# Modulation, x and the first products of a two-block transformer kernel, pair by pair instead of all at once

## The reference

```python
c_act = jax.nn.silu(c)                                     # (1, 1024)
mod = jnp.einsum('bd,de->be', c_act, w_ada[l]) + b_ada[l]   # (1, 6 * 1024)
sh1, sc1, g1, sh2, sc2, g2 = [m[:, None, :] for m in jnp.split(mod, 6, axis=-1)]
h = x * (1.0 + sc1) + sh1
proj = jnp.einsum('bsd,dk->bsk', h, w_in)
z, xbc, dt_raw, q, k, v, f_raw = jnp.split(proj, SPLITS, axis=-1)
```

## Time and profile before

| | |
|---|---|
| median of 3 runs | 1414.13 us (1413.6 to 1414.81) |
| the profiled execution, its own time | 1416.64 us |
| its span (first to last instruction) | 1414.9 us |
| instructions | 17285 |
| DMA | 158.58 MB, mean 112 GB/s |

### The profile page before, as it was taken

The page is one execution under the profiler, slowest core; times in us unless marked ns, Lnnn a source line. Parts: engine busy times, 40 slices in busy tenths (PEclk is TensorE's granted clock), DMA queues, the critical chain, the costliest instruction groups (busy, mean ns, idle before and its releaser), DMA issues.

```text
span 1414.9 us, 17285 instructions
## 1 busy us (share of the span) xinstructions
PE 1368.2 (97%) x6567; PEld 1123.8 (79%) x6567; DVE 692.2 (49%) x1005; ACT 547.8 (39%) x793; POOL 690.8 (49%) x544
## 2 busy tenths in 40 slices
PE   2999999999999999999999997999999999999999
PEld 2888788888878778888888886887788888888887
DVE  6676978789753672131325456348623213132231
ACT  0636445566663252231332316325525323142230
POOL 0453855432346664455445544754644445445442
PEclk9999999999999999999999999999999999999999
DMA  9353435655323433322232232343132322322231
GB/s 334 119 131 101 98 119 179 194 152 167 105 72 132 139 90 111 97 89 90 93 114 89 89 110 72 100 122 89 46 119 67 112 89 89 115 93 89 89 104 74
DMA packets 132248, 158.58 MB, mean 112 GB/s; under 512 B 9468, under 2 KB 93712, under 8 KB 131936
## 3 DMA queue, kind: packets, MB, share of 16 engines
q1 hardware_dynamic: 123760, 146.95, 33.2%
q10 hardware_dynamic: 6240, 5.40, 1.6%
q0 software_dynamic: 2192, 5.49, 1.2%
HBM read 153.47 MB, written 2.26 MB: 110 GB/s over the span
## 4 chain that ended last, share of the span: by engine, by line
PE 88%; DVE 5%; POOL 3%; ACT 1%; issue 1%; DMA 1%; SPq 0%; DVEq 0%; POOLq 0%; ACTq 0%
PE bank L1706 26%; PE bank L1707 26%; PE bank L1708 26%; POOL w_lo L551 3%; DVE tmp L1271 2%; PE bank L1845 2%; PE bank L1855 1%; DMA arena<-in_w_ada_dram 1%; PE bank L2223 1%; PE bank L2038 1%; PE bank L1830 1%; PE bank L1858 1%; PE bank L1820 1%; PE bank L2039 1%; PE bank L1982 1%
## 5 line engine op out<-in xcount | busy, mean ns | idle before, releaser
L551 POOL TENSOR_TENSOR w_lo<-raw,w_hi 128x512 fp32r<-128x512 f32 x428 | 588.5, 1407 | 601.1 <-ACT w_hi L745 599.9
L1706 PE MATMUL bank<-w_hi,a_hi 128*128 128x512 f32 x928 | 364.6, 393 | 8.3 <-DVE a_lo L1164 6.0
L1708 PE MATMUL bank<-w_hi,a_lo 128*128 128x512 f32 x928 | 361.9, 390 | 0.0
L1707 PE MATMUL bank<-w_lo,a_hi 128*128 128x512 f32 x928 | 361.9, 390 | 0.0
L745 ACT ACTIVATE w_hi<-raw 128x2048 fp32r<-128x2048 f32 x107 | 204.5, 1911 | 365.3 <-PE bank L1708 361.7
L1706 PE MATMUL bank<-a_hi,w_hi 128*128 128x512 f32 x800 | 316.4, 395 | 3.4 <-DVE a_lo L1164 2.5
L1707 PE MATMUL bank<-a_lo,w_hi 128*128 128x512 f32 x800 | 312.9, 391 | 0.0
L1708 PE MATMUL bank<-a_hi,w_lo 128*128 128x512 f32 x800 | 312.8, 391 | 0.0
L1706 PEld LDWEIGHTS bank<-w_hi,a_hi 128*128 128x128 f32 x928 | 174.7, 188 | 46.2 <-DVE a_lo L1164 6.2
L1708 PEld LDWEIGHTS bank<-w_hi,a_lo 128*128 128x128 f32 x928 | 174.6, 188 | 36.8
L1707 PEld LDWEIGHTS bank<-w_lo,a_hi 128*128 128x128 f32 x928 | 174.7, 188 | 35.5
(11 more groups left out here) (248 smaller groups left out, 1246.7 us busy)
## 6 DMA issues: line engine op xcount, KB each, us to landing
raw<-in_w_mlp_dram SPq DMA_DIRECT2D x32, 1024.0 KB, 5.2
raw<-in_w_in_dram SPq DMA_DIRECT2D x24, 1024.0 KB, 5.2
arena<-in_w_ada_dram SPq DMA_DIRECT2D x18, 1024.0 KB, 6.7
raw<-in_w_ff_in_dram SPq DMA_DIRECT2D x16, 1024.0 KB, 5.4
raw<-in_w_ff_out_dram SPq DMA_DIRECT2D x16, 1024.0 KB, 5.0
raw<-in_w_out_dram SPq DMA_DIRECT2D x12, 1024.0 KB, 5.3
raw<-in_w_in_dram SPq DMA_DIRECT2D x16, 512.0 KB, 5.6
arena<-in_w_ada_dram SPq DMA_DIRECT2D x3, 2048.0 KB, 17.9
```

The costliest lines, as they stand in the source:

```text
L551: last = pool.tensor_tensor(w_lo[:, u0 % 2, cols], raw[:, u0 % 2, cols], w_hi[:, u0 % 2, cols].bitcast(F32), ALU.subtract)
L1706: pe.matmul(out_, hi_a, hi_b, start=start, stop=False)
L1707: pe.matmul(out_, hi_a, lo_b, start=False, stop=False)
L1708: return pe.matmul(out_, lo_a, hi_b, start=False, stop=stop)
```

## The change

The early columns of w_ada are loaded and used in four pieces g = 0 to 3. Piece g holds 256 columns of shift and the 256 columns of scale for the same features, that is for feature tiles 2g and 2g + 1. It comes in four DMAs (upper and lower four row blocks, shift and scale), and the quarter of x with the same features comes ahead of it. Unit U_XBC and the time step's columns come between pieces 0 and 1.

On each engine the work goes pair by pair. DVE weighs piece g, waits for PE's column sums, makes four columns of `mod`, and makes `a_lo` of the two tiles; the casts of unit U_XBC stand behind the first weighing. ACT waits for its part of `mod` and makes `a_hi` and the rests of the two tiles. PE sums the columns of piece g, transposes the next quarter of x (into banks 3 to 6, used twice), and multiplies the two tiles: time step, n = 0 and n = 1. Bank 7 holds the sums. The result of a weighing lies in a buffer of its own (`weighed`) instead of `tmp`.

```diff
+X_BANKS = (3, 4, 5, 6, 3, 4, 5, 6)
+        weighed = view(17280, 2, 512)
 (SP, prelude)
-                for half in range(2):
-                    sp.dma_start(ada[:, 0, 4 * half:4 * half + 4], w_ada_v[:, 4 * half:4 * half + 4, 0:512]).then_inc(ada_half[half], 16)
-                for n in range(1, 4):
-                    sp.dma_start(ada[:, n], w_ada_v[:, :, n * 512:n * 512 + 512]).then_inc(ada_in[n], 16)
-                sp.dma_start(xtok, x_v).then_inc(x_in, 16)
-                columns(0, 0, U_XBC, w_in_v, C_XBC + P * XBC_ORDER[0])
-                sp.wait_ge(cleared, 3)
-                sp.dma_start(dt_raw[:, :, 0:16], w_in_v[:, :, C_DT:C_DT + 16]).then_inc(dt_in, 16)
-                sp.dma_start(dt_raw[:, :, 32:48], w_in_v[:, :, C_F:C_F + 16]).then_inc(dt_in, 16)
+                for g in range(4):
+                    sp.dma_start(xtok[:, :, 256 * g:256 * g + 256], x_v[:, :, 256 * g:256 * g + 256]).then_inc(x_in[g], 16)
+                    for half, signal in enumerate((ada_upper[g], ada_lower[g])):
+                        rows_ = slice(4 * half, 4 * half + 4)
+                        for m in range(2):
+                            col = 1024 * m + 256 * g
+                            sp.dma_start(ada[:, g, rows_, 256 * m:256 * m + 256], w_ada_v[:, rows_, col:col + 256]).then_inc(signal, 16)
+                    if g == 0:
+                        columns(0, 0, U_XBC, w_in_v, C_XBC + P * XBC_ORDER[0])
+                        sp.wait_ge(cleared, 3)
+                        sp.dma_start(dt_raw[:, :, 0:16], w_in_v[:, :, C_DT:C_DT + 16]).then_inc(dt_in, 16)
+                        sp.dma_start(dt_raw[:, :, 32:48], w_in_v[:, :, C_F:C_F + 16]).then_inc(dt_in, 16)
 (ACT)
-            act.wait_ge(mod_made, 1)
-            turned_affine(R_H, T_H, 0, lambda k: mod[:, 8 + k:9 + k], lambda k: mod[:, k:k + 1])
+            def first_rest(k):
+                act.wait_ge(a_hi_made, T_H + k + 1)
+                if k >= 2:
+                    act.wait_ge(a_lo_made, T_H + k - 1)
+                act.activation(tmp[:, k % 2], a_hi[0][:, k].bitcast(F32), ACT.Identity, scale=-1.0, bias=mod[:, k:k + 1]).then_inc(tile_made, 1)
+            for g in range(4):
+                act.wait_ge(mod_made, g + 1)
+                for k in (2 * g, 2 * g + 1):
+                    turned_hi(R_H, 0, k, X_BANKS[k], mod[:, 8 + k:9 + k], mod[:, k:k + 1])
+                    if k % 2:
+                        first_rest(k - 1)
+                first_rest(2 * g + 1)
             hi(U_XBC + 1)
 (DVE, start)
-                (one weigh per piece n, sums of all four, then mod, the casts of U_XBC, split_affine)
+                for g in range(4):
+                    before = [(ada_upper[g], 32)] + ([(col_mm, g - 1)] if g >= 2 else [])
+                    weigh(weighed[:, g % 2], lambda k: ada[:, g, k], before, ada_sum, (ada_lower[g], 32))
+                    if g == 0:
+                        dve.wait_ge(vecs_t, 1)
+                        dve.tensor_copy(vec[:].rearrange("p a b -> p (a b)"), bank[7][:, 0:256]).then_inc(vecs_made, 1)
+                        dve.wait_ge(vecs_made, 1)
+                        dve.wait_ge(landed[U_XBC % 2], 16)
+                        for half in range(2):
+                            cols = slice(1024 * half, 1024 * half + 1024)
+                            dve.tensor_copy(w_hi[:, U_XBC % 2, cols], raw[:, U_XBC % 2, cols]).then_inc(w_hi_made, 1)
+                    dve.wait_ge(col_mm, g + 1)
+                    sums, v = bank[7][:, 256 + 4 * g:260 + 4 * g], V_BADA + 2 * g
+                    dve.tensor_tensor(mod[:, 2 * g:2 * g + 2], sums[:, 0:2], v0[:, v:v + 2], ALU.add)
+                    dve.scalar_tensor_tensor(mod[:, 8 + 2 * g:10 + 2 * g], sums[:, 2:4], 1.0, v0[:, v + 8:v + 10], ALU.add, ALU.add)\
+                        .then_inc(mod_made, 1)
+                    for k in (2 * g, 2 * g + 1):
+                        dve.wait_ge(tile_made, M_H + k + 1)
+                        dve.scalar_tensor_tensor(a_lo[0][:, k], bank[X_BANKS[k]][:], mod[:, 8 + k:9 + k], tmp[:, k % 2], ALU.mult, ALU.add)\
+                            .then_inc(a_lo_made, 1)
 (PE; the loop over m and the 32 transposes in one go are gone)
+            def turn_x(g):
+                pe.wait_ge(x_in[g], 16)
+                if g >= 2:
+                    pe.wait_ge(a_lo_made, T_H + 2 * g - 2)
+                turn(xtok, 2, 2 * g, X_BANKS)
+            def first_products(g):
+                if g == 0:
+                    pe.wait_ge(dt_made, 1)
+                for k in (2 * g, 2 * g + 1):
+                    pe.wait_ge(a_lo_made, T_H + k + 1)
+                    last = three(bank[0][0:DT_W, :], dt_hi[:, k], dt_lo[:, k], a_hi[0][:, k], a_lo[0][:, k], k == 0, k == KT - 1)
+                    if k in (3, 7):
+                        last.then_inc(ticks, 1)
+                    if k % 2 == 0:
+                        if g < 2:
+                            pe.wait_ge(x0_lo, g + 1)
+                        else:
+                            pe.wait_ge(w_lo_made, g - 1)
+                    for n in range(2):
+                        last = column_step(U_XBC, n, 0, bank[XBC_BANK[n]][:], k)
+                        if k == KT - 1:
+                            last.then_inc(ticks, 1)
+            turn_x(0)
+            (then the transposes of the small vectors, as before)
+            for g in range(4):
+                pe.wait_ge(ada_sum, g + 1)
+                if g:
+                    pe.wait_ge(mod_made, g)
+                sum_columns(weighed[:, g % 2], 7, 256 + 4 * g, 4, col_mm)
+                if g < 3:
+                    turn_x(g + 1)
+                first_products(g)
```

More of the change, by code:

```diff
@@ L265, in build @@
         c_in, c_t, dt_in = sem("c_in"), sem("c_t"), sem("dt_in")
-        x_in, small_in, mod_made = sem("x_in"), sem("small_in"), sem("mod_made")
-        ada_in = [None] + [sem(f"ada_in{n}") for n in range(1, 4)]
-        ada_half = [sem("ada_half0"), sem("ada_half1")]
+        x_in, small_in, mod_made = [sem(f"x_in{g}") for g in range(4)], sem("small_in"), sem("mod_made")
+        ada_upper, ada_lower = [sem(f"ada_upper{g}") for g in range(4)], [sem(f"ada_lower{g}") for g in range(4)]
         late_in = [sem("late_in0"), sem("late_in1")]
@@ L1283, in start @@
                 dve.wait_ge(c_made, 1)
[L1284 to L1297, removed]
@@ L1298, in start @@
-                split_affine(M_H, 0, lambda k: mod[:, 8 + k:9 + k])
+                for g in range(4):
[18 more added lines that the diff above has]
+                            .then_inc(a_lo_made, 1)
```

## The result

The changed kernel takes 1421.7 us (median of 5 runs, 1419.65 to 1423.05), beside 1414.17 us before (5 runs): ratio 1.0047, 95% interval 1.0036 to 1.0058. In a second session it was 1422.54 (ratio 1.0054, 1.0039 to 1.0069). The change makes the kernel slower by half a per cent. The forecast was 1420.4, 0.45% more.

A forecast was written before the change was run, and what follows sets the result against it. PE, busy 97% of the span, was taken as the bound, so its start moves the end. 5.73 + 0.3 (POOL) + 0.3 (clock) gave +6.3 us on the median 1414.13: 1420.4 us, range 1417.0 to 1423.4.

The forecast's parts named there:

- the post: PE's first matmul with weight unit U_XBC + 1: forecast 62.39 us instead of 56.66, +5.73, before the unseen costs.
- three signs of error: Rounds shorter than 10 us, DVE waiting for loads in pairs 1 to 3, or PE not waiting for w_lo after first products.
- M0: Pair 0's mod signal, the first: forecast at 16.77 us instead of 35.42, a gain of 18.7.
- Pair 1: Its weighing on DVE was to begin at 20.5 us, 1.5 after its upper piece landed at 19.0.
- The second rival: Early loads slowed by 1 KB rows: at 300 GB/s, 2.1 us more, 1422.5 us; chance 0.08.
- POOL beside the weighing: POOL's w_lo parts of unit U_XBC slow pair 1's weighing: 0.3 us taken, from none to 1.0.
- The rounds: Mod signal to mod signal, one pair: 11.92 us, with DVE's next weighing behind its waits for PE and ACT.
- bound (c): PE's column sums 1 to 3 at the high clock: 0.8 us less each, up to 2.4 back; none taken.
- M3: Pair 3's mod signal, the last: forecast at 52.53 us, after three rounds of 11.92.
- The end: U_XBC + 1's low part, cast behind ACT's last rest, ends last: PE waits until 62.39 us, its products ending at 59.7.
- The clock's term: PE's matmuls of pair 3 partly at the low clock after gaps: 0.3 us taken, bounds 0 and 1.4.
- the first rival: DVE's waits not holding up the next pair's weighing: 8 us faster, 1406; chance 0.06.

The follow-up runs named there:

- e4: Changed kernel with DVE weighing the next pair before this pair's a_lo, and PE summing it before this pair's products: 1416.84 us, ratio 1.0012.
- e10: Kernel before, only its early w_ada and x loads cut into 1 KB rows, in more DMAs: 1418.1 us, ratio 1.0024.
- e1: Changed kernel with ACT's cast of unit U_XBC + 1 moved ahead of pair 3's activations: 1425.54 us, ratio 1.0076.
- a0: Changed kernel, unaltered, run again in a second session: 1422.54 us, ratio 1.0054 to the kernel before.
- e2: Changed kernel plus 2, 5, 9 and 12 unread extra matmuls on PE ahead of the pairs' products: 1423.25 us, ratio 1.0060.
- e12: Changed kernel with U_XBC + 1's cast ahead of pair 3's activations, held until the last weighing ends, plus 2, 4, 7, 9 extra matmuls: 1419.7 us, ratio 1.0041.
- e8: e4 with U_XBC + 1's cast ahead of pair 3's activations, held until the last weighing ends: 1413.7 us, ratio 0.9988; repeated, 1413.98, 0.9995.
- e11: e8 with SP's time-step loads behind pair 1's pieces, time-step cast and subtraction later: 1413.55 us, ratio 0.9988.
- e5: Changed kernel with POOL instead of SP issuing the two time-step loads: 1422.72 us, ratio 1.0059.

## Why the prediction was right, and where its steps were not

The sum for the post was 5.73 + 0.6 = 6.3 us and the profile shows 6.18; the median moved by 7.5, to 1421.7, inside the range. The main mechanism holds: DVE's order keeps each pair's weighing behind the waits of the one before, and e4, which changes only that order and PE's to match, gives back 5.7 us. But several terms were off by up to 2.3 us, and they cancelled: that the sum came within 0.2 us is luck. Of the three signs of error that the prediction names, two came: DVE waited for a load in pair 1, and PE went on without a wait for w_lo. The third, rounds below 10 us, did not.

- *M0, 16.77 forecast, 19.06 measured.* Pair 0's pieces were taken up at 10.1 and 13.4 instead of 8.0 and 10.8, and this put M0 late. Two steps were wrong. The smaller one is "all pieces now have rows of 1 KB ... so I charge nothing": the full stream ran at 350 GB/s, and e10, with the same rows and pieces in the old order, at 346. By 10.10 us the changed kernel's stream had moved 246 GB/s against 263 before, which is worth only 0.5 us. I had read 384 GB/s from a 2 us window inside one isolated load, where nothing but the middle of it was seen. The larger one is the rule that a piece has landed as soon as the bytes up to its end have passed: 2.4 MiB had passed when the first 1.5 were there, and at 350 GB/s the 0.9 MiB between are 2.6 us. The rule fitted the first MiB of both kernels (6.6 us) and, within 0.5 us, the next pieces of the kernel before (taken up at 9.84 and 15.41, by the rule 9.4 and 14.9), but not those of the changed kernel. Why loads issued later get so large a share is open; the width of the rows, the number of DMAs and their order all changed together. The Trainium skill (Perfetto Trace Analysis, DMA Optimizations) says that DMAs below 2 KB carry a significant overhead. e10's 346 against 378 agrees with it if a row of 1 KB counts as such a DMA, but e10 can't tell the rows from the number of DMAs.
- *Pair 1, forecast 1.5 us after its load, waited 0.47 for it.* I had priced the time-step loads by their time in the stream (1.3) and not by SP's issue of them; its upper piece was there at 23.0 instead of 19.0. The second rival was thus half true: the stream was slow, but its landing times stopped mattering from pair 2 on, where DVE waited for no load.
- *POOL beside the weighing, 0.3 forecast.* The first operation of pair 1 took 1.47 instead of 0.48, beside the end of POOL's parts (19.29 + 4.96 = 24.25): 1.0, my high end. e1 prices it for a full weighing: 3.6.
- *The rounds, 11.92 forecast, 10.81 measured.* PE's sums took 1.05 instead of 1.86 from pair 1 on (bound (c)), for PE's clock was high at those moments (a weight load of the sums took 0.192 there and 0.333 in pair 0); from mod to the last a_lo it was 3.53 instead of 3.70. This took back 2.2 us in two rounds, so that M3 came at 53.03, against 52.53.
- *The end.* The low part was ready at 62.59, forecast 62.39. I had named as a sign of error that PE goes on without a wait for w_lo, and it did: 13 of pair 3's 18 matmuls ran at the low clock, and the products ended 0.25 us past the low part. In a0's execution the low part came last, by some 0.2 us. The clock's term, 0.3, had the right size; e2 and e12 show the two chains one behind the other.
- *Smaller slips.* Fourteen more DMAs stand ahead of the next unit's load, not ten; it was issued at 34.0 and stayed hidden. The price of the first rival, 8 us faster, let M3 come at 38.7. It left out the arrival of the pieces and that pair 0 can't have its mod before 16.77 by the prediction's own sum. With that rival made true (e4) M3 came at 46.1, and its best descendant (e8) is within about a tenth of a per cent of the kernel before.

The median moved by 7.5 us, the profiled span by 6.4. The profiled execution of before lay 2.5 us above its median, that of the changed kernel 1.35 above its own, and this is the difference. The profiled executions also differ far behind the change: before, changed and e10 ran for some 7 us between 188 and 202 us at a granted clock of 0.50, and none of the others did. What decides this is open.

Open: whether DVE's wait for ACT (2.1 to 2.6 us at the last pair, in every version that goes by pairs) can be shortened; no version here tried that.

## What to carry to other kernels

Work cut into pairs overlaps only if the engine that starts the next pair does so before it waits for the others; write its queue in that order, or each round costs the whole round trip. When a step is moved to an engine's free time, look at what the other engines do at that moment: the same cast lost 3 us in one place and gained 3 in another. Price a load by a long window of loads like it, by what its issue holds up in the queue, and by when such a load landed and not only by the bytes ahead of it.

## What was unexpected of the hardware

- DVE's weighing and POOL's subtractions slow each other: 5.48 to 9.05 us for seven, 4.98 to 6.32 us for POOL's four (e1). DVE's a_lo, with an operand in PSUM, was not slowed: in the changed kernel the two of pair 0 took 1.41 us at 21.18, beside the POOL row below, as did the two of pair 3 with POOL idle.

```profile
19.29 4.96 POOL L633 TENSOR_TENSOR w_lo<-raw,w_hi 128x512 fp32r<-128x512 f32 x4
```

- A load can land well behind its bytes: 2.4 MiB had passed when the first 1.5 MiB were there (changed kernel, 10.1 us).
- Issuing two loads of 64-byte rows, 64 KB each, took SP 4.13 + 3.61 us in the changed kernel, 8.08 + 3.33 before, 1.46 + 2.87 in e11, and 1.13 + 0.92 on POOL's queue in e5. So the rows alone don't set it. What was already queued is the likely rest, which no run isolates.
- The granted clock column reads 1.00 in the prelude even where PE ran at the low level: in the changed kernel the window of 24 to 25 us says 1.00, and this row of it lasted as long as the slow one at 60.71 (0.63).

```profile
24.24 0.63 PE L1729 MATMUL bank<-a_hi,w_lo 128*128 128x512 f32 x1
```
